# GpSimd's mask additions in pieces of 256 columns in two attention mixers

## The reference, cut to what matters

```python
# first block, neighbourhood attention, per row of the 64-wide grid
col_in = (col[None, :] >= col_start[:, None]) & (col[None, :] < col_start[:, None] + kw)
s = s + jnp.transpose(bias, (0, 2, 1, 3)).astype(jnp.float32)[None]
s = jnp.where(col_in[None, None, :, None, :], s, MASK_VALUE)

# second block, forgetting attention, per block of 128 queries
s = s + ci[..., :, None] - c[:, :, None, :]
s = jnp.where(kpos[None, :] <= qpos[:, None], s, -jnp.inf)
```

## Time and profile before

| what | value |
|---|---|
| time, median of 3 runs | 810.64 us (808.24 to 811.5) |
| the profiled execution's own time | 808.22 us |
| its span in the trace | 806.4 us |
| TensorE, products | 757.0 us busy, 94% of the span |
| TensorE, weight loads | 537.7 us, 67% |
| VectorE | 408.5 us, 51% |
| ScalarE | 311.3 us, 39% |
| GpSimd | 24.6 us, 3% |
| chain that ended last | TensorE 78%, DMA 11%, VectorE 6%, ScalarE 3% |

### The profile page before, as it was taken

One profiled execution on the slowest core, in us unless ns is written; L12 is line 12 of the kernel. 1 busy time (PEld: TensorE's weight loads), 2 busy tenths in 40 slices (PEclk: granted clock), 3 DMA queues, 4 the chain that ended last, 5 costly groups with the idle time before them and its releaser, 6 DMA issues.

```text
span 806.4 us, 11672 instructions
## 1 busy us (share of the span) xinstructions
PE 757.0 (94%) x4551; PEld 537.7 (67%) x4554; DVE 408.5 (51%) x728; ACT 311.3 (39%) x554; POOL 24.6 (3%) x22
## 2 busy tenths in 40 slices
PE   4999999998997999999999889999899999999997
PEld 2497785443694443453354257887698999999885
DVE  2583704579646121121121146767556788888543
ACT  3463203556625011010010035645445666665433
POOL 0000120022000000000000000020000000000000
PEclk9999999999999999999999988999998999999999
DMA  9882113976399989999999994205302544585301
GB/s 375 343 321 112 60 45 116 357 272 243 161 366 371 382 348 421 421 423 422 421 421 421 421 427 186 106 0 210 130 2 105 190 147 185 208 334 219 126 0 53
DMA packets 22698, 198.96 MB, mean 247 GB/s; under 512 B 2528, under 2 KB 2912, under 8 KB 4224
## 3 DMA queue, kind: packets, MB, share of 16 engines
q1 hardware_dynamic: 21744, 194.80, 60.2%
q0 software_dynamic: 624, 3.28, 1.0%
q10 hardware_dynamic: 288, 0.30, 0.1%
HBM read 197.32 MB, written 1.05 MB: 246 GB/s over the span
## 4 chain that ended last, share of the span: by engine, by line
PE 78%; DMA 11%; DVE 6%; ACT 3%; issue 1%; SPq 0%; DVEq 0%; ACTq 0%
PE banks L1511 10%; PE banks L1101 8%; PE banks L1787 7%; PE banks L1762 6%; PE banks L1766 5%; PE banks L1770 5%; PE banks L1545 4%; DMA ring<-in_w_gate 3%; DMA ring<-in_w_up 3%; PE banks L1059 3%; DMA ring<-in_w_in 3%; PE banks L1298 2%; PE banks L1479 2%; DMA ring<-in_w_mod 2%; DVE w_lo L1836 2%; PE banks L1127 2%
## 5 line engine op out<-in xcount | busy, mean ns | idle before, releaser
L1836 DVE TENSOR_TENSOR w_lo<-ring,w_hi 128x1024 fp32r<-128x1024 f32 (+1 forms) x122 | 145.9, 1202 | 81.9 <-ACT w_hi L678 30.8
L1511 PE MATMUL banks<-ring,att 128*64 128x512 f32 x512 | 115.3, 594 | 8.9 <-DMA ring<-in_w_up 5.3
L1511 PEld LDWEIGHTS banks<-ring,att 128*64 128x64 f32 x512 | 41.9, 137 | 80.4 <-issue 65.8
L678 ACT ACTIVATE w_hi<-ring 128x1024 fp32r<-128x1024 f32 x50 | 51.9, 1053 | 35.5 <-PE banks L1101 23.4
L2200 DVE TENSOR_TENSOR lat<-lat,banks 128x512 f32<-128x512 f32 x8 | 5.5, 687 | 104.7 <-PE banks L1511 104.7
L1545 PE MATMUL banks<-ring,lat 128*64 128x512 f32 x224 | 50.3, 597 | 2.9 <-DVE lat L2202 2.9
L1762 PE MATMUL banks<-h_hi,w_hi 128*128 128x256 f32 x352 | 51.6, 286 | 0.6 <-ACT h_hi L994 0.5
L971 ACT ACTIVATE w_hi<-ring 128x1024 fp32r<-128x1024 f32 x44 | 46.2, 1052 | 14.3 <-PE banks L1770 14.3
L1766 PE MATMUL banks<-h_hi,w_lo 128*128 128x256 f32 x352 | 50.2, 286 | 0.0
L1770 PE MATMUL banks<-h_lo,w_hi 128*128 128x256 f32 x352 | 49.9, 285 | 0.0
L1762 PEld LDWEIGHTS banks<-h_hi,w_hi 128*128 128x128 f32 x352 | 45.9, 192 | 2.1 <-ACT h_hi L994 1.2
(11 more groups left out here) (363 smaller groups left out, 1430.0 us busy)
## 6 DMA issues: line engine op xcount, KB each, us to landing
ring<-in_w_gate SPq DMA_DIRECT2D x32, 1024.0 KB, 14.2
ring<-in_w_up SPq DMA_DIRECT2D x32, 1024.0 KB, 16.2
ring<-in_w_down SPq DMA_DIRECT2D x29, 1024.0 KB, 16.8
ring<-in_w_mod SPq DMA_DIRECT2D x11, 2048.0 KB, 8.3
ring<-in_w_up SPq DMA_DIRECT2D x11, 2048.0 KB, 7.8
ring<-in_w_in SPq DMA_DIRECT2D x8, 2048.0 KB, 16.7
ring<-in_w_down SPq DMA_DIRECT2D x5, 2048.0 KB, 10.8
ring<-in_w_out SPq DMA_DIRECT2D x4, 2048.0 KB, 7.8
```

Of the source, the lines that this page charges most:

```text
L678: nc.scalar.activation(chunk_part(w_hi, chunk, c), chunk_src(chunk, c), ACT.Copy).then_inc(chunk_hi[stage], 1)
L1511: last = nc.tensor.matmul(bank[2 + j][CAP * e:CAP * (e + 1), :], xs[:, k, at:at + CAP], slot(n + e, KD)[:, k, :], start=(k == 0), stop=(k ...
L1836: return V.tensor_tensor(dst, src, high.bitcast(F32), ALU.subtract)
```

## The change

Each of GpSimd's four large additions is cut into pieces of 256 columns. The two additions of the bias become eight pieces each (four rows of 64 columns times 64), the two additions of `tri` four pieces each (two heads of 128 columns): 24 instructions stand where 4 stood. Only the last piece of each run raises the semaphore; waits, data, order and transfers are as before.

```diff
                 b = arena[:, 2048 * half:2048 * (half + 1)].rearrange("p (a n) -> p a n", n=GRID_W)
-                nc.gpsimd.tensor_tensor(b, b, namask.unsqueeze(1).broadcast_to([P, 32, GRID_W]),
-                                        ALU.add).then_inc(bias_ready, 1)
+                for i in range(0, 32, 4):
+                    ins = nc.gpsimd.tensor_tensor(b[:, i:i + 4, :], b[:, i:i + 4, :],
+                                                  namask.unsqueeze(1).broadcast_to([P, 4, GRID_W]), ALU.add)
+                ins.then_inc(bias_ready, 1)
                 pool.wait_ge(bias_ready, half + 1)
...
-            nc.gpsimd.tensor_tensor(nck0[:, :, :], nck[:, :, 0:P], tri.unsqueeze(1).broadcast_to([P, H, P]),
-                                    ALU.add).then_inc(nck_done, 1)
+            for h in range(0, H, 2):
+                ins = nc.gpsimd.tensor_tensor(nck0[:, h:h + 2, :], nck[:, h:h + 2, 0:P],
+                                              tri.unsqueeze(1).broadcast_to([P, 2, P]), ALU.add)
+            ins.then_inc(nck_done, 1)
             pool.wait_ge(nck_done, 1)
-            nc.gpsimd.tensor_tensor(nck[:, :, P:T], nck[:, :, P:T], tri.unsqueeze(1).broadcast_to([P, H, P]),
-                                    ALU.add).then_inc(nck_done, 1)
+            for h in range(0, H, 2):
+                ins = nc.gpsimd.tensor_tensor(nck[:, h:h + 2, P:T], nck[:, h:h + 2, P:T],
+                                              tri.unsqueeze(1).broadcast_to([P, 2, P]), ALU.add)
+            ins.then_inc(nck_done, 1)
```

## The result

The changed kernel takes 803.27 us (median of 4 executions, 802.88 to 804.79) beside 810.75 us for the kernel before (4 executions, 808.24 to 811.5). The ratio is 0.9917, 95% interval 0.9892 to 0.9942. It is faster, by under 1% but clear of noise: by 7.5 us where 3.5 were forecast; 803.27 lies under the range's lower end of 805.0. The profiled execution took 803.42 us, where the prediction's own sum for it was 804.7, with a span of 801.6, 4.8 us under the span before.

A forecast was written before the change was run, and what follows sets the result against it. The prediction took TensorE to bound most of the span, stalled twice in the first attention by scalings shut out by GpSimd's additions. Gains 1.26 + 2.53 - 0.3 = 3.5 us gave 810.64 - 3.5 = 807.1 us, range 805.0 to 810.8.

The forecast's parts named there:

- The bound, the place and the mechanism of the stalls: First attention: two VectorE scalings stand over 4 us each because GpSimd's bias additions hold the shared SBUF ports; TensorE idles.
- The sum of the first attention: Gains of 1.26 us at the first stall and 2.53 at the second, less 0.3: 3.5 us, ends 2.5 and 3.8.
- The 0.3 for late second scalings: Second stall of the first attention: scalings waiting for pieces in flight cost 0 to 1.3 us together, taken as 0.3.
- The mask in time: First attention: the first half's pieces end by 171.4 us at worst, VectorE wants them at 173.4, so no wait.
- The second mask: GpSimd's additions there end up to 0.2 us late; cost 0 to 0.4 us, taken as nothing.
- Is the gain kept: Behind the attention: weight issues follow TensorE's progress, so full transfers start equally earlier and the 3.5 us stay.
- Rival (b): Experts' stage: transfers are the limit from the start and eat the gain, time 810.6 us; chance 0.10.
- Rival (a): GpSimd keeps the ports between pieces, so a scaling stands for the whole run: 814.9 us; chance 0.08.
- Rival (d): Second mask late by 0.4 us for TensorE, and the whole 1.3 us lost in the first attention: 808.6 us; chance 0.08.
- rival (c): TensorE's clock stays up at 211 us once the stalls are gone, saving 1.9 us more: 805.2 us; chance 0.14.

The follow-up runs named there:

- first mixer alone: Against the kernel before, GpSimd's additions cut into pieces in the first mixer only, the second mixer left as before: ratios 0.9934 and 0.9931, 803.11 ± 0.38 us.
- no addition: Against the kernel before, the first mixer's mask added only to the first 64 of each 2048 columns: ratio 0.9934, stretch 89.52 us.

## Why the prediction was too small, point by point

**The bound, the place and the mechanism of the stalls were right.** Taking the addition away and cutting it give the same 89.5 us, so it was the addition that made the two stalls, and nothing else in this stretch was waiting behind them.

**The sum of the first attention** was 1.26 + 2.53 - 0.3 = 3.5 us; measured 3.80, in that stretch. The two terms add up to 3.79. The 0.3 for late second scalings was not needed: a piece takes 0.69 us from start to start (0.70 assumed between 0.57 and 0.83; 163.60 to 164.98 us holds two), a scaling waits up to 0.5 us for it, and the scalings of 182.79 end 0.5 us and more before their transposes at 185.17.

**The mask in time:** right. The first half is ready at 168.15 us and wanted at 171.76.

**The second mask:** right, with less in hand than before. GpSimd ends at 526.88 + 2.83 = 529.71 and is wanted at 530.71, 1.0 us later (1.9 before). VectorE's subtraction there takes 1.52 us where it took 1.21, and TensorE's stretch is unchanged.

```profile
529.26 1.52 DVE L1842 TENSOR_TENSOR w_lo<-ring,w_hi 128x1024 fp32r<-128x1024 f32 x1
530.71 0.35 DVE L2045 SCALAR_TENSOR_TENSOR banks<-banks,small,arena 128x128 f32<-128x128 f32 x1
```

**Is the gain kept:** right. From the first expert weights to the second block nothing is given back, within 0.1 us; in the stretch of full transfers 3.80 us went through as they were. Rival (b) falls. Rival (a) falls for pieces of 256 and of 1024, where no scaling waited for more than one piece. As a mechanism it is real all the same, as the scaling at 188.87 in the kernel with pieces of 64 shows. Rival (d) falls with the unchanged 51.5 us of the second mask's stretch and the 3.80 us of the first attention's.

**Two terms of the sum failed: the clock, put at nothing, and the time that the gain was taken from.** The forecast was 810.64 - 3.5, with the clock left out but for rival (c), one fall at one place, worth 1.9 us, with a chance of 0.14.

First, the clock. All kernels without the long stalls (changed, first mixer alone, no addition; n = 34) have a mean of 802.85 ± 0.25 us and a shortfall of 14.02 ± 0.33. Against the kernel before that is 5.5 ± 0.3 us, 1.7 over the 3.8 of the stretch, and 1.5 ± 0.4 less shortfall. Filling the stalls' idle time gives 1.35 ± 0.37 us by itself, 0.2 to 0.3 of it from a slightly shorter stretch. That leaves 1.1 ± 0.4 of the 1.7 as clock (0.9 ± 0.4 against the executions beside them); the remaining 0.6 is about one standard error.

Second, the starting time. 810.64 us was the median of three executions. The mean of 74 is 808.37, and they lie between 804.1 and 811.9 us. The text gave medians a spread of about 1 us, which went into the chances and not into the range. The 7.5 us are then 3.8 from the stretch, 1.7 more in the means, and 2.0 from the draw: 810.75 is 2.4 over the mean of its kernel, 803.27 is 0.4 over that of the kernels without the long stalls. From 808.37 the forecast's 3.5 would have given 804.9 and the 5.5 give 802.9; the measured 803.27 lies 0.4 from the second.

That rival (c) comes to 5.4 us in all, close to 5.5, is luck. In the pair of profiles its place did save 1.64 us, but the kernel before, profiled once more, takes 17.97 us in that stretch as the changed one does, and loses 1.7 us in the next. The argument against (c), that the idle 1.12 us stay where they are, was no argument either: in the changed kernel they stayed and the clock was up (1.95 us for the product behind them), and filling them brought nothing.

**What stays open.** Why the clock falls for longer in some executions is not settled; where it does, the profiles show. Read microsecond by microsecond, the granted clock is 1.00 from 28 to 206 us in all fourteen profiles, so there is no fall in the stalls nor in the 20 us after them. The falls lie at 18 to 27 us, at 207 to 214 or 252 to 261, at 471 to 493, 567 to 580, 598 to 619 and in the last 4 us. Some places are hit in each profile and some only in a part of them, and their length differs. The stretches differ accordingly: ahead of the attention (94.7 to 96.5 us), between the first expert weights and the second pair (60.9 to 61.0, or 59.3), around 450 to 500 us (53.9 or 52.3), 555 to 615 us (61.0 to 64.1) and from there to the end (188.0 to 190.0). Of the six profiles with a stall that idles or is filled five have the fall in the second of these; of the eight without it four. That is a leaning, not a finding. If the stalls cost clock, as the means say, they do it from a distance, and by what is not shown.

A straight line within each kernel's executions (0.70 us of time for each us of shortfall) puts the changed kernel 4.5 ± 0.2 us under the kernel before at equal clock, 0.7 more than the stretch shows. The same line puts the kernel with pieces in the second mixer alone 0.5 ± 0.2 under, though its stretch is no shorter. I take the line to be too crude for that remainder, but this was only argued.

## What to carry to other kernels

A short VectorE instruction that was slow twice among 32, with no semaphore behind it, pointed here at a GpSimd instruction that was running: look at maximum against median, line by line. The remedy was the piece size, and it must be such that every waiting instruction can afford one piece each: half the length gained nothing here where a pair of scalings stood in a row, an eighth gained everything. Then look at the maximum again: pieces of 64 went ahead of a waiting scaling once, four in a row. GpSimd's longer total costs nothing until its result is wanted; here 32 pieces a half were still in time, by 0.6 us.

A gain of 1% wants more than three executions of the kernel before: here the median of three lay 2.3 us over the mean of 74.

## What the runs showed of the hardware that was not expected

- GpSimd and VectorE took turns at the ports also when GpSimd had its next piece ready: with pieces of 256 columns the scalings at 182.79 take 1.84 us for two, with pieces of 1024 one takes up to 2.60. It is no rule: with pieces of 64 one scaling took 1.72 us and was served only after GpSimd's last piece.
- An addition of 64 columns takes 0.317 us and of 256 columns 0.73 undisturbed; from start to start it is 0.30 and 0.69. The fixed part that a run of pieces pays is about 0.17 us each (0.69 - 256 x 2.06 ns = 0.16; 0.30 - 0.13 = 0.17), about half of what a line through single instructions of 1024 and 2048 gave (0.30).
- The same idle 1.30 us ahead of the same product (568.07 and 575.19) stood beside a fall of the clock in both profiled kernels, yet the changed kernel, 7.1 us ahead by then, stayed at the lower level 6.4 us longer (until 577.7, against 578.4 in the kernel before).
- TensorE kept busy with products of zeros in 3 us of stalls made an 808 us kernel 1.35 ± 0.37 us faster, 1.1 ± 0.4 of it beyond what the stretch gives; in 0.9 us of idle time elsewhere nothing shows.
